# Where the experts' buffers start in their partitions: 96 bytes past a multiple of 512 in place of 384

## The chip, the cores and the metric

One core of a Trainium2 chip runs the whole program in one launch. The metric is the device time of that launch in microseconds, the median of several executions.

## The reference, cut to what matters

The program computes two blocks on a sequence of 256 tokens of width 1024, all in float32. The first block has two layers of mLSTM and retention; the second has two layers of convolution and banded attention, each followed by a feed-forward part, which is dense in the first layer and a mixture of eight experts in the second. The mixture is the part that the change touches:

```python
logits = t @ w_router + b_router            # t: 256 x 1024, 8 experts
top_val, top_idx = lax.top_k(logits, 2)
combine = sum(one_hot(top_idx) * softmax(top_val))
for e in range(8):
    out += combine[:, e:e+1] * ((silu(t @ w_gate[e]) * (t @ w_up[e])) @ w_down[e])
```

w_gate[e] and w_up[e] are 1024 x 3584, w_down[e] is 3584 x 1024. One expert has 42 MiB of weights, all eight 336 MiB.

## The kernel before, in words

**Split products.** Each float32 product is computed as three products of the type float32r. An operand x is split into a high part (x cast to float32r) and a low part (x minus the high part), and high by high, low by high and high by low are summed in PSUM. Weights come in units of 1 MiB, 2048 floats in each of 128 partitions: SP loads a unit into one of the slots of `raw` (line 529), ScalarE casts it to `whi` (line 739), VectorE subtracts to get `wlo` (line 1781), and TensorE multiplies. `whi` and `wlo` have three slots each. A unit is cast two units ahead of TensorE, and its cast waits until TensorE is done with the unit that held the slot.

**The experts.** For each expert, at most 128 chosen tokens are gathered (lines 1626 and 1648) into `xghi` and `xglo`. 28 units hold gate and up weights, 14 hold down weights. In both parts the tokens are the stationary operand, 128x128, and the weights are the moving one, 512 columns wide; each unit takes 12 products:

```python
mm(o, xghi[:, k, x], whi[:, u.hl, w], start=k == 0, stop=False)      # line 1682
mm(o, xglo[:, k, x], whi[:, u.hl, w], start=False, stop=False)       # line 1683
last = mm(o, xghi[:, k, x], wlo[:, u.hl, w], ...)                    # line 1684
```

Lines 1713 to 1715 are the same for down, with `thi` and `tlo` (the gated rows, turned by TensorE in line 1668 and taken out of PSUM by lines 1108 and 2451) as the stationary operand. That makes 8 x 28 x 12 = 2688 products of gate and up and 8 x 14 x 12 = 1344 of down, 4032 together. The result of an expert, scaled, is split into `ehi` and `elo` and spread back to the tokens' places with `pickT` as the moving operand, 256 columns (lines 1656 and 1657). An extra pass for experts with more than 128 tokens exists and runs only if there are such.

**Everywhere else** the weights are mostly the stationary operand, 128x128, and activations the moving one, 256 columns: `hhi` and `hlo` in lines 1161 to 1163, `yhi`, `fhi` and `y2hi` and their low parts in lines 1216 to 1218. In lines 1202 to 1204 the roles are the other way round, also with 256 columns. The sums of squares in line 1233 and the transposes are plain float32.

**Places.** Buffers are allocated one behind the other in each partition by `sb(...)`, and stacks that are closed give their place back, so later stages lie over earlier ones. Some small buffers (`half_line_h`, `half_line_c`, `half_line_y`, 32 bytes each) hold nothing and only move what follows. Worked out from the sizes, the starts modulo 512 bytes are: `raw`, `whi`, `wlo` 128; `hhi`, `hlo` 160; `acc` and `pickT` 192; `yhi`, `fhi`, `y2hi` and their low parts 224; `thi`, `tlo`, `htok`, `xghi`, `xglo`, `mg`, `ma`, `pick`, `ehi`, `elo` 384. Each slice that a product reads starts a whole number of 512 bytes behind its buffer's start, so every product has its buffers' residues. Taking the moving operand's start minus the stationary one's, modulo 512, gives one number for each family of products:

| products | moving | stationary | difference |
|---|---|---|---|
| 1161-1163 | `hhi`, 256 columns | `whi` | +32 |
| 1202-1204 | `whi`, 256 | `hhi` | -32 |
| 1216-1218 | `yhi`, `fhi`, `y2hi`, 256 | `whi` | +96 |
| 1648 | `pick`, 256 | `hhi` (tokens) | +224 |
| 1656, 1657 | `pickT`, 256 | `ehi`, `elo` | +320 |
| 1682-1684, 1713-1715 | `whi`, `wlo`, 512 | `xghi`, `thi` | +256 |

**Order.** Each engine's order is written out by hand and kept by semaphores; no planner decides it. `lrow`, a 256-float buffer for the router's logits, lies in `acc[:, 2]`; ScalarE writes it (line 1071) and TensorE reads it (line 1610) once, before the experts.

Of the kernel before, what the change touches and what calls it, by code (L numbers as in the profile page):

```python
# [5 lines left out]
F32 = mybir.dt.float32  # L6
# [6 lines left out]
P = 128  # L13
S = 256
# [24 lines left out]
FE = 3584  # L39
# [20 lines left out]

UW = 2048
HALF_LINE = 8
RAW = 6
HALF = 3
MOE_SLOTS = (3, 4, 5, 2, 0, 1)
# [32 lines left out]
S_MOE = S_B3 + UNIT_L2  # L98
assert S_MOE % HALF == 2 and A_MIX1 + ADA_MIX[1] == ADA_UNITS and (2 * HEAD_UNITS) % HALF == 0 and JOB_UNITS % RAW == 0 and JOB_UNITS % HL == 0 and ADA_TURN[0] % HALF == 0 and ADA_TURN[1] % HALF == 0
FREE0, DONE0 = HALF, 1  # L100
# [25 lines left out]
class Unit:  # L126
# [17 lines left out]
    @property  # L144
    def raw(self):
        return self.n % HALF if self.n < S_MOE else MOE_SLOTS[(self.n - S_MOE) % RAW]

    @property
    def loads(self):
        slots = HALF if self.n < S_MOE else RAW  # L150
        if self.n < S_MOE:
            first = self.n // HALF
        else:
            first = (self.n - S_MOE) // RAW + ((S_MOE + HALF - 1 - self.raw) // HALF if self.raw < HALF else ADA_UNITS // HALF - sum(HALF + i % HALF == self.raw for i in ADA_SPARE))
        return self.turn * (16 * self.per // slots) + (16 * first + 16) if self.per else 16 * first + 16
# [104 lines left out]
def two_block_model(nc, x, positions, consts, c, w_ada, b_ada, norm_g, w_in, conv_w, conv_b, b_igate, b_fgate,  # L260
# [7 lines left out]
    with ctx:  # L268
        def sb(name, shape, dt=F32, stack=ctx):
            return stack.enter_context(nc.sbuf_tensor(name, shape, dt))  # L270

        def sem(name):
            return ctx.enter_context(nc.semaphore(name))


        raw = sb("raw", [P, RAW, UW])
        whi = sb("whi", [P, HL, UW], F32R)
# [3 lines left out]

        sb("half_line_h", [P, HALF_LINE])
        hhi = sb("hhi", [P, KD, S], F32R)
        hlo = sb("hlo", [P, KD, S], F32R)
        sb("half_line_c", [P, HALF_LINE])
        cst = sb("cst", [P, C_BEFORE])
# [16 lines left out]
        acc = sb("acc", [P, HALF, S], F32, ba)  # L303
        sb("half_line_y", [P, HALF_LINE], F32, ba)

# [89 lines left out]
        ba.close()  # L395
        bm = ExitStack()
        pickT = sb("pickT", [P, S], F32R, bm)
        sb("rest_of_acc", [P, 2 * S + HALF_LINE], F32, bm)
        sb("half_line_t", [P, 5 * HALF_LINE], F32, bm)
        thi = sb("thi", [P, FE // P, P], F32R, bm)  # L400
        tlo = sb("tlo", [P, FE // P, P], F32R, bm)
        htok = sb("htok", [P, 2, D], F32, bm)
# [2 lines left out]
        mg = sb("mg", [P, 2, 512], F32, bm)  # L405
# [2 lines left out]
        moe = h  # L408
        wr = sb("wr", [P, KD, NE], F32, bm)
        rb = sb("rb", [P, 1], F32, bm)  # L410
        lrow = acc[:, 2]
        lg = rstd[:, 0:24 * NE].rearrange("p (a t e) -> p a t e", a=12, t=2)
        comb = sb("comb", [P, 2, NE + 1], F32, bm)
        combhl = sb("combhl", [P, 2, NE + 1, 2], F32R, bm)
# [5 lines left out]
        otok, hthi, htlo = (x[:, :, :].rearrange("p (t k) s -> p t (k s)", t=2) for x in (h, hhi, hlo))  # L420
        bm.close()
        be = ExitStack()
        sb("before_htok", [P, S + 2 * S + HALF_LINE + 5 * HALF_LINE + 2 * FE], F32, be)
        ehi = sb("ehi", [P, D], F32R, be)
        elo = sb("elo", [P, D], F32R, be)
        be.close()
# [17 lines left out]

        raw_in = [sem(f"raw_in{i}") for i in range(RAW)]
        c_in, rows1_in = sem("c_in"), sem("rows1_in")
# [2120 lines left out]
```

How the kernel before makes its waits and increments, by code:

```python
    def wait(self, back=0):  # L247
        v = self.n - back
        self.eng.wait_ge(self.sem, self.turn * self.per + v if self.per else v)
# [269 lines left out]
        @block.sync  # L519
# [6 lines left out]
            def load(u, src, k):  # L526
                sp.wait_ge(raw_free, u.free(1 - (HALF if u.n < S_MOE else RAW)))
                sp.dma_start(raw[:, u.raw, :].rearrange("p (k n) -> p k n", k=k), src).then_inc(raw_in[u.raw], 16)
# [1 line left out]
            def ada_load(a, block, l, at):  # L531
                if a.n >= ADA_START:
                    last = Ada(a.n - HALF, 0)
                    if ADA_START <= last.n < A_MIX0 or A_FF <= last.n < A_MIX1:
                        sp.wait_ge(ada_free, last.sums())
                    else:
                        sp.wait_ge(ada_done, last.count())
                elif a.n >= HALF:
                    sp.wait_ge(ada_done, a.n - HALF - len(ADA_SPARE) + 1)
                w = (w_ada, w_ada_2)[block][l].rearrange("(k p) n -> p k n", p=P)
                sp.dma_start(raw[:, a.raw, :].rearrange("p (k n) -> p k n", k=KD), w[:, :, bass.ds(at * 256, 256)])\
                    .then_inc(raw_in[a.raw], 16)
# [64 lines left out]
                        load(u, w[:, 4 * half:4 * half + 4, 512 * c:512 * c + 512], 4)  # L608
                    else:
                        f = 2 * (j - JOB_UP)
                        load(u, wd[:, f:f + 2, :], 2)
            sp.wait_ge(ada_done, ADA_UNITS)
            with sp.Fori(0, NE) as e:
                job_loads(e, e, S_MOE, range(JOB_UNITS))
```

## Time and profile before

| | us |
|---|---|
| median of three executions | 2103.86 (2103.12 to 2104.84) |
| profiled execution, its own time | 2104.48 |
| span of the profiled execution | 2102.6 |
| TensorE busy | 2055.7 (98%) |
| VectorE busy | 1766.0 (84%) |
| ScalarE busy | 1322.5 (63%) |
| mean transfer rate over the span | 283 GB/s |

The profile lists, for each engine, how long it was busy; a chain of waits from the last instruction back to the first; groups of equal instructions with their mean duration; and the data transfers. Durations of matrix products run from a product's start to its modelled end, and products overlap: the next one starts before the former one's end. How far apart starts are is read from the start times. The experts' stage runs from about 1117 us to 2089 us of the span.

### The profile page before, as it was taken

Reading aid. Unit: us, or ns where it says so; the run is one execution under the profiler, and the core shown is the slowest. Engines: PE = TensorE matmul, PEld = TensorE weight load, DVE = VectorE, ACT = ScalarE, POOL = GpSimd, SP = SyncE. Lnnn points to the kernel's source line nnn. Section 1 sums busy time; section 2 is a strip of 40 time slices with the busy share of each in tenths; the row PEclk is TensorE's granted clock in tenths of the full one; section 3 lists DMA queues with packets and bytes.
Section 4 is the critical chain, followed back from the end, with each engine's and each line's share of the span. In section 5 each row is a group of like instructions: output and inputs, shape, how many; then the busy total and the mean of one; then the engine's idle time right before and its main releaser. Section 6 shows DMA issues by size and latency. Waiting matters only on the chain.

```text
span 2102.6 us, 33818 instructions
## 1 busy us (share of the span) xinstructions
PE 2055.7 (98%) x13569; PEld 1833.1 (87%) x13569; DVE 1766.0 (84%) x2185; ACT 1322.5 (63%) x1265; POOL 30.5 (1%) x60
## 2 busy tenths in 40 slices
PE   7999999999999999999999999999999999999998
PEld 5999999999999889999878888888888888888887
DVE  4898976888759878888878888898898889898887
ACT  3655655566645663435757777777777777777774
POOL 3000000000000000000000000000000000000000
PEclk8999999999999999999999999999999999999999
DMA  9887865676656369987447999999999999999994
GB/s 297 252 260 239 250 211 161 221 220 198 216 183 218 128 213 307 312 323 227 141 164 268 360 354 360 373 367 344 362 358 374 361 343 367 368 365 355 355 359 187
DMA packets 356161, 595.07 MB, mean 283 GB/s; under 512 B 10376, under 2 KB 201368, under 8 KB 356008
## 3 DMA queue, kind: packets, MB, share of 16 engines
q1 hardware_dynamic: 352864, 586.92, 80.8%
q0 software_dynamic: 2752, 5.86, 1.1%
q8 instruction: 110, 1.80, 0.4%
q14 instruction: 43, 0.35, 0.0%
q10 hardware_dynamic: 392, 0.13, 0.0%
HBM read 591.80 MB, written 4.22 MB: 283 GB/s over the span
## 4 chain that ended last, share of the span: by engine, by line
PE 85%; DVE 8%; ACT 3%; DMA 2%; issue 2%; SPq 0%; POOL 0%; DVEq 0%; POOLq 0%; ACTq 0%
PE ps L1682 9%; PE ps L1684 9%; PE ps L1683 9%; PE ps L1161 6%; PE ps L1163 6%; PE ps L1162 6%; PE ps L1715 5%; PE ps L1714 5%; PE ps L1713 5%; PE ps L1216 3%; PE ps L1217 3%; PE ps L1218 3%; DVE wlo L1781 2%; PE ps L1202 1%; PE ps L1203 1%
## 5 line engine op out<-in xcount | busy, mean ns | idle before, releaser
L1781 DVE TENSOR_TENSOR wlo<-raw,whi 128x2048 fp32r<-128x2048 f32 x485 | 1108.6, 2287 | 190.4 <-ACT whi L739 189.8
L739 ACT CAST whi<-raw 128x2048 fp32r<-128x2048 f32 x485 | 926.5, 1911 | 363.2 <-PE ps L1684 123.6
L1161 PE MATMUL ps<-hhi,whi 128*128 128x256 f32 x1360 | 388.0, 285 | 0.5 <-DVE wlo L1781 0.5
L1163 PE MATMUL ps<-hhi,wlo 128*128 128x256 f32 x1360 | 380.4, 280 | 0.0
L1162 PE MATMUL ps<-hlo,whi 128*128 128x256 f32 x1360 | 380.3, 280 | 0.0
L1682 PE MATMUL ps<-whi,xghi 128*128 128x512 f32 x896 | 354.6, 396 | 0.8 <-DVE wlo L1781 0.8
L1684 PE MATMUL ps<-wlo,xghi 128*128 128x512 f32 x896 | 349.7, 390 | 0.0
L1683 PE MATMUL ps<-whi,xglo 128*128 128x512 f32 x896 | 349.1, 390 | 0.0
L1161 PEld LDWEIGHTS ps<-hhi,whi 128*128 128x128 f32 x1360 | 256.5, 189 | 7.6 <-issue 7.3
L1162 PEld LDWEIGHTS ps<-hlo,whi 128*128 128x128 f32 x1360 | 256.5, 189 | 0.3
L1163 PEld LDWEIGHTS ps<-hhi,wlo 128*128 128x128 f32 x1360 | 256.4, 189 | 0.0
L1684 PEld LDWEIGHTS ps<-wlo,xghi 128*128 128x128 f32 x896 | 168.2, 188 | 36.0
L1682 PEld LDWEIGHTS ps<-whi,xghi 128*128 128x128 f32 x896 | 168.3, 188 | 34.4 <-DVE wlo L1781 2.4
L1683 PEld LDWEIGHTS ps<-whi,xglo 128*128 128x128 f32 x896 | 168.5, 188 | 32.2
L1713 PE MATMUL ps<-whi,thi 128*128 128x512 f32 x448 | 175.2, 391 | 0.0
L1715 PE MATMUL ps<-wlo,thi 128*128 128x512 f32 x448 | 174.9, 390 | 0.0
L1714 PE MATMUL ps<-whi,tlo 128*128 128x512 f32 x448 | 174.6, 390 | 0.0
L1837 DVE SCALAR_TENSOR_TENSOR acc<-raw,cact,acc 128x256 f32<-128x256 f32 x324 | 132.7, 477 | 0.0
L1715 PEld LDWEIGHTS ps<-wlo,thi 128*128 128x128 f32 x448 | 84.1, 188 | 17.7
L1714 PEld LDWEIGHTS ps<-whi,tlo 128*128 128x128 f32 x448 | 84.1, 188 | 17.0
L1713 PEld LDWEIGHTS ps<-whi,thi 128*128 128x128 f32 x448 | 84.1, 188 | 16.9
L1202 PE MATMUL ps<-whi,hhi 128*128 128x256 f32 x320 | 91.8, 287 | 0.0
(407 smaller groups left out, 3011.5 us busy)
## 6 DMA issues: line engine op xcount, KB each, us to landing
raw<-in_moe_w_gate_dram SPq DMA_DIRECT2D x112, 1024.0 KB, 6.2
raw<-in_moe_w_up_dram SPq DMA_DIRECT2D x112, 1024.0 KB, 6.4
raw<-in_moe_w_down_dram SPq DMA_DIRECT2D x112, 1024.0 KB, 5.1
raw<-in_w_in_dram SPq DMA_DIRECT2D x92, 1024.0 KB, 5.4
raw<-in_w_ada_dram SPq DMA_DIRECT2D x69, 1024.0 KB, 7.8
raw<-in_w_out_dram SPq DMA_DIRECT2D x24, 1024.0 KB, 5.1
raw<-in_ffn_w_gate_dram SPq DMA_DIRECT2D x11, 1024.0 KB, 9.1
raw<-in_ffn_w_up_dram SPq DMA_DIRECT2D x11, 1024.0 KB, 9.1
```

Of the source, the lines that this page charges most:

```text
L739: nc.scalar.copy(whi[:, u.hl, :], raw[:, u.raw, :]).then_inc(hi_ready, 1)
L1161: mm(ps2[u.bank][:, j], whi[:, u.hl, w], hhi[:, k], start=k == 0, stop=False)
L1162: mm(ps2[u.bank][:, j], whi[:, u.hl, w], hlo[:, k], start=False, stop=False)
L1163: last = mm(ps2[u.bank][:, j], wlo[:, u.hl, w], hhi[:, k], start=False, stop=k == KD - 1)
L1682: mm(o, xghi[:, k, x], whi[:, u.hl, w], start=k == 0, stop=False)
L1683: mm(o, xglo[:, k, x], whi[:, u.hl, w], start=False, stop=False)
L1684: last = mm(o, xghi[:, k, x], wlo[:, u.hl, w], start=False, stop=k == KD - 1)
L1713: mm(o, thi[:, f], whi[:, u.hl, w], start=f == 0, stop=False)
L1714: mm(o, tlo[:, f], whi[:, u.hl, w], start=False, stop=False)
L1715: last = mm(o, thi[:, f], wlo[:, u.hl, w], start=False, stop=f == FE // P - 1)
L1781: V.tensor_tensor(wlo[:, u.hl, :], raw[:, u.raw, :], whi[:, u.hl, :].bitcast(F32), ALU.subtract).then_inc(raw_free, 1)
L1837: last = V.scalar_tensor_tensor(sums[k % 2], w[:, k], cact[:, block, k:k + 1], sums[k % 2], ALU.mult, ALU.add)
```

## The change

All buffers of the experts' stage that lie behind `pickT` begin 288 bytes earlier modulo 512 (1824 bytes earlier in all): at 96 in place of 384. The two unused buffers between `pickT` and `thi` (520 + 40 floats) become one of 104 floats. `pickT` stays at 192, the weights at 128. `ehi` and `elo`, which lie over `htok`, move with it. As `thi` now covers the place of `acc[:, 2]`, `lrow` is put into the first 256 floats of `mg`. The difference of the experts' products (moving minus stationary) becomes 128 - 96 = +32, that of lines 1656 and 1657 +96, that of line 1648 96 - 160 = -64. No instruction, wait or order is added, taken away or moved.

```diff
 HALF_LINE = 8
+T_PAD = 104
 RAW = 6
...
         pickT = sb("pickT", [P, S], F32R, bm)
-        sb("rest_of_acc", [P, 2 * S + HALF_LINE], F32, bm)
-        sb("half_line_t", [P, 5 * HALF_LINE], F32, bm)
+        sb("before_thi", [P, T_PAD], F32, bm)
         thi = sb("thi", [P, FE // P, P], F32R, bm)
...
-        lrow = acc[:, 2]
+        lrow = mg[:, 0, 0:S]
...
         be = ExitStack()
-        sb("before_htok", [P, S + 2 * S + HALF_LINE + 5 * HALF_LINE + 2 * FE], F32, be)
+        sb("before_htok", [P, S + T_PAD + 2 * FE], F32, be)
         ehi = sb("ehi", [P, D], F32R, be)
```

## Rows read from the trace of the kernel before

**Rows 1.** The page: engine shares, the 40 slices, the chain's shares by engine.

```profile
PE 2055.7 (98%) x13569; PEld 1833.1 (87%) x13569; DVE 1766.0 (84%) x2185; ACT 1322.5 (63%) x1265; POOL 30.5 (1%) x60
...
PE   7999999999999999999999999999999999999998
...
PE 85%; DVE 8%; ACT 3%; DMA 2%; issue 2%; SPq 0%; POOL 0%; DVEq 0%; POOLq 0%; ACTq 0%
```

**Rows 2.** Busy time in two stretches: experts, down part (us, engines, clock, DMA share, GB/s).

```profile
1117.00:2089.00 972.00, 970.31 (x4504) 804.84 (x4504) 862.62 (x544) 704.38 (x474) 0.00 (x0) 1.00 0.98 355
1325.00:1355.00 30.00, 30.00 (x134) 24.82 (x134) 25.80 (x13) 21.07 (x11) 0.00 (x0) 1.00 1.01 378
```

**Rows 3.** Waits from 1200 to 2050 us: waiting instruction, releaser, total us, times, longest.

```profile
ACT whi L739 <- PE ps L1684: 108.2, 139, 1.6
DVE wlo L1781 <- ACT whi L739: 95.5, 159, 1.4
ACT whi L739 <- PE ps L1715: 88.8, 97, 1.9
```

**Rows 4.** The experts' product groups of the page: busy us, mean ns, idle before.

```profile
L1682 PE MATMUL ps<-whi,xghi 128*128 128x512 f32 x896 | 354.6, 396 | 0.8 <-DVE wlo L1781 0.8
L1684 PE MATMUL ps<-wlo,xghi 128*128 128x512 f32 x896 | 349.7, 390 | 0.0
L1683 PE MATMUL ps<-whi,xglo 128*128 128x512 f32 x896 | 349.1, 390 | 0.0
L1713 PE MATMUL ps<-whi,thi 128*128 128x512 f32 x448 | 175.2, 391 | 0.0
L1715 PE MATMUL ps<-wlo,thi 128*128 128x512 f32 x448 | 174.9, 390 | 0.0
L1714 PE MATMUL ps<-whi,tlo 128*128 128x512 f32 x448 | 174.6, 390 | 0.0
```

**Rows 5.** TensorE from 1504 to 1511 us: start us, duration us, product.

```profile
1504.21 0.39 PE L1682 MATMUL ps<-whi,xghi 128*128 128x512 f32 x1
...
1507.38 0.39 PE L1684 MATMUL ps<-wlo,xghi 128*128 128x512 f32 x1
1507.62 0.60 PE L1668 MATMUL ps<-cst,ma 128*128 128x128 f32 x4
1507.97 0.48 PE L1682 MATMUL ps<-whi,xghi 128*128 128x512 f32 x1
1508.28 0.40 PE L1683 MATMUL ps<-whi,xglo 128*128 128x512 f32 x1
...
1510.14 0.39 PE L1682 MATMUL ps<-whi,xghi 128*128 128x512 f32 x1
```

**Rows 6.** Products by line: duration ns min/median/max, first and last start us.

```profile
L1684 PE MATMUL ps<-wlo,xghi x896: 387/389/398, 1111.3 to 2050.1; 128*128 128x512 f32 x180
L1715 PE MATMUL ps<-wlo,thi x448: 388/389/398, 1192.0 to 2088.7; 128*128 128x512 f32 x150
L1161 PE MATMUL ps<-hhi,whi x1360: 277/280/470, 48.1 to 1041.6; 128*128 128x256 f32 x195
L1204 PE MATMUL ps<-wlo,hhi x320: 274/280/288, 56.8 to 1025.1; 128*128 128x256 f32 x160
L1218 PE MATMUL ps<-fhi,wlo x176: 278/282/286, 900.2 to 966.8; 128*128 128x256 f32 x176
L1648 PE MATMUL ps<-pick,hhi x64: 278/282/283, 1198.0 to 1960.0; 128*128 128x256 f32 x64
L1656 PE MATMUL ps<-pickT,ehi x64: 279/282/419, 1256.9 to 2092.9; 128*128 128x256 f32 x64
```

**Rows 7.** TensorE: a stretch of 256-column products, and one of plain float32.

```profile
564.18 0.28 PE L1163 MATMUL ps<-hhi,wlo 128*128 128x256 f32 x1
...
566.98 0.28 PE L1163 MATMUL ps<-hhi,wlo 128*128 128x256 f32 x1
...
636.85 3.62 PE L1233 MATMUL ps<-h,gsq 128*128 128x256 f32 x16
```

**Rows 8.** VectorE's subtraction of 512 columns at either residue: busy us, mean ns.

```profile
L2451 DVE TENSOR_TENSOR tlo<-ps,thi 128x512 fp32r<-128x512 f32 x56 | 38.2, 683 | 0.0
L2314 DVE TENSOR_TENSOR flo<-fa,fhi 128x512 fp32r<-128x512 f32 x11 | 7.5, 684 | 0.0
```

## The prediction

> **What bounds the kernel now.** I read the page's busy shares first, then the chain, then the experts' stage by itself, and last the single products. The page shows TensorE busy for 98% of the span in all 40 slices and 85% of the chain on it [rows 1]. In the experts' stage, 972 us long, TensorE is busy for 970.31 us at full clock, and VectorE for 862.62 us, 89% [rows 2]. The waits say who leads: ScalarE's cast waits for TensorE to give a slot back, 197 us in total in that stage, and the largest of the others is VectorE's wait for the cast; no cast waits for a transfer [rows 3]. So a nanosecond more or less on each of the experts' products arrives in the end time nearly whole, and nothing else that the change touches can.
>
> Busy time hides how fast products follow each other, so I take starts. In rows 5, from 1504.21 to 1507.38 us there are 14 steps: 3.17 us / 14 = 226.4 ns from start to start, with durations of 389 ns. Duration minus step is 163 ns. The 256-column products show the same difference: 24 steps from 564.18 to 566.98 us are 116.7 ns each, under a median of 280 [rows 7, 6]. Plain float32 products too: 16 of them take 3.62 us, their last start lies 3.62 - 0.38 = 3.24 us behind the first, 216 ns a step, at 379 ns each [rows 7]. So I read a duration minus 163 as the cost of a product in a stream, and can use the groups' durations as a ruler at one nanosecond. Over 4032 products, one nanosecond is 4.0 us of the kernel.
>
> **The change part by part.** It takes away no instruction and no wait. What it can alter is how the reads of the moving operand and of the next stationary operand meet in a partition, which depends on the difference of their places.
>
> *The experts' 4032 products, difference +256 to +32.* The median is 389 ns, the least 387 [rows 6]: most of them run in one settled rhythm, 226.4 ns. Does the settled rhythm depend on the difference? No row shows 512 columns at +32, so I bound it by the 256-column families. Their medians are 280 at +32, 280 at -32, 282 at +96, +224 and +320 [rows 6], so the difference is worth about 2 ns there. Their shortest, apart from one at 274, are 277 to 279, that is 114 to 116 ns a step. Half of the experts' 226.4 is 113.2: for each column they are already as fast as the quickest products of any family at any difference. I take that as a floor that the place does not move, and the settled rhythm as unchanged: 0 us.
>
> *The unsettled ones.* After the transposes the rhythm is disturbed: from 1508.28 to 1510.14 us 8 steps take 1.86 us, 232.5 ns each [rows 5]. The six groups are busy for 354.6 + 349.1 + 349.7 + 175.2 + 174.9 + 174.6 = 1578.1 us [rows 4]; 4032 x 0.389 = 1568.4; 9.7 us are above the settled duration. Of these, 56 products that follow a transpose directly last about 0.48 us, 0.09 more than 0.39 [rows 5]: 5.0 us, which is the transposes' own time. The rest, 4.7 us, is what the disturbed rhythm costs. With another difference it can go to nothing, or become the rule: all products at 232.5 would cost 4032 x 6.1 = 24.6 us. The bounds are thus -4.7 and +24.6 us while the floor holds, and I take 0, since the row nearest to it is the settled one, at which most of the stage runs now.
>
> If the floor does not hold, the nearest lower row is plain float32 at 216 ns: 10.4 x 4032 = 41.9 us less.
>
> *The 128 spreading products (+320 to +96) and the 128 gathering ones (+224 to -64).* The families differ by 2 ns in their medians [rows 6], so 256 x 2 = 0.5 us either way; taken as 0.
>
> *ScalarE and VectorE* write the moved buffers at an odd multiple of 32 bytes in place of a multiple of 64. `flo` already lies so (224) and `tlo` does not (384), and VectorE takes 684 and 683 ns for them [rows 8]: 0. If ScalarE's or VectorE's pieces grew by 1%, they have slack: VectorE's 862.62 of 972 us [rows 2]. The transfers of weights keep their places. `lrow` in `mg` is written and read once, by the same instructions behind the same waits, and `mg` is first used by the experts afterwards: 0.
>
> The sum is 0 with bounds of -42.4 and +25.1 us (both with the 0.5). The profiled execution took 2104.48 us, its span 2102.6 and 1.9 around it; the median is 2103.86, 0.6 lower, and I apply the sum to the median: 2103.9.
>
> Two rules of the Trainium skill bear on this. The page SBUF — State Buffer (section "SBUF: two separate sides") says that TensorE has ports of its own and never waits on another engine, and in its table of paths that the weight load has a second, independent read port. By that rule no difference of places could cost anything. The trace does not quite agree: the same products at the same clock last 389 ns or up to 398 [rows 6], depending on what ran before them. The page TensorE: Matmul & The Clock Gate (section "Back-to-back issue gap") gives N/2.4 + 2.5 ns at full clock, an estimate of 215.8 ns for 512 columns. [...]
>
> **The rivals.** The reader can tell them apart by the median duration alone.
>
> *Slower: at +32 the rhythm does not settle.* The place is every expert product; the mechanism is that the load of the next tokens and the moving weights meet again in each product. For it: the only family at +32 does not run at its own shortest, 277, but at 280 in the median, 3 ns more [rows 6], while at +256 the experts show no such excess. Carried over, 4032 x 3 = 12.1 us: 2116. At the disturbed 232.5 ns it would be 2128. Against it: with 512 columns the weight load has twice the time, and the disturbed rhythm was seen to die out. It decides from 1 ns a product on.
>
> *Faster, a little: the difference carries over as it stands.* At +32 the 256-column products are 2 ns better than at +96, +224 and +320. If +256 is like these and half-hidden in the 389, the experts gain 2 to 3 ns: 8 to 12 us, 2094. Against it: at -32 the median is 280 as well, and the floor argument above.
>
> *Faster, much: the floor is no floor.* 41.9 us less, 2062, if all the excess over plain float32 goes. VectorE would then be busy for 862.6 of 930 us, 93%, and the transfers run at 355 x 972/930 = 371 GB/s, below the 378 that the down part shows [rows 2], so neither forbids it. Against it: none of the five 256-column families comes near half of 216.
>
> **How the numbers follow.** Forecast, rhythm unchanged: 0.45. Slower: 0.28. A little faster: 0.19. Much faster: 0.08. A change of less than 0.2%, 4.2 us, is what a measurement of this kernel can hardly tell from none. The forecast's own range is 2099 to 2109; I leave 0.02 of its chance beyond 4.2 us on either side. So faster is 0.19 + 0.08 + 0.02 = 0.29, same 0.41, slower 0.28 + 0.02 = 0.30. The range is 2090 to 2120: it takes in the little gain and the 12.1 us loss, and leaves out the much faster case (0.08) and the fully disturbed one (some 0.07).
>
> **What would show it.** Right: lines 1684 and 1715 keep a median of 389 ns, the six groups' busy time stays within 5 us of 1578.1, and the experts' stage is 968 to 976 us long. The slower rival shows a median of 392 or more; the faster ones 386 to 387, or 379. The counts of rows 6 for lines 1161 and 1218 must not move at all. If the six groups' sum changes by more than 5 us and the end time does not follow, my reading that nothing waits beside TensorE is wrong; if the time moves with all durations as before, something outside the products did it.

## The result and the profile after

The changed kernel is slower: 2124.43 us in the median of four executions (2123.39 to 2125.58) against 2103.99 for the kernel before beside it. The ratio is 1.0100, 95% interval 1.0087 to 1.0112. The forecast was 2103.9 with a range of 2090 to 2120, so the time lies outside it, on the side of the rival "at +32 the rhythm does not settle". Of all executions of the kernels below, one, of e9_even256, ran at a lower mean granted clock than the rest (0.92 in place of 0.99) and took 2137.23 us; it is in the ratio given there.

The page of the kernel after, to be laid beside [rows 1]:

```profile
span 2121.5 us, 33818 instructions
PE 2075.2 (98%) x13569; PEld 1830.6 (86%) x13569; DVE 1766.7 (83%) x2185; ACT 1321.6 (62%) x1265; POOL 30.5 (1%) x60
```

The instructions are as many as before. VectorE's and ScalarE's busy times are within 1 us of what they were; TensorE is busy for 2075.2 us in place of 2055.7, 19.5 more, and the span is 18.9 longer. The experts' stage alone, as in [rows 2], ends 18.5 us later (the last product of line 1715 starts at 2107.2 us, before at 2088.7) and has hardly a gap in TensorE's time:

```profile
1117.00:2107.00 990.00, 989.37 (x4494) 802.45 (x4493) 860.70 (x542) 701.70 (x472) 0.00 (x0) 1.00 0.98 348
```

The six groups of [rows 4] in the kernel after (line, products, count, busy us, mean ns, idle before):

```profile
L1682 PE MATMUL ps<-whi,xghi 128*128 128x512 f32 x896 | 358.7, 400 | 0.6 <-DVE wlo L1781 0.6
L1684 PE MATMUL ps<-wlo,xghi 128*128 128x512 f32 x896 | 353.9, 395 | 0.0
L1683 PE MATMUL ps<-whi,xglo 128*128 128x512 f32 x896 | 353.7, 395 | 0.0
L1713 PE MATMUL ps<-whi,thi 128*128 128x512 f32 x448 | 177.7, 397 | 0.0
L1714 PE MATMUL ps<-whi,tlo 128*128 128x512 f32 x448 | 176.9, 395 | 0.0
L1715 PE MATMUL ps<-wlo,thi 128*128 128x512 f32 x448 | 176.9, 395 | 0.0
```

They sum to 1597.8 us against 1578.1: 19.7 us, which is the whole of the loss within what the two profiles can tell. (Counted from the first expert product to the last, the stage is 21.1 us longer; it began 2.6 us earlier in this execution.) Every group has grown by 4 to 6 ns in its mean. The durations by line, beside [rows 6]:

```profile
L1684 PE MATMUL ps<-wlo,xghi x896: 388/396/400, 1108.7 to 2067.6; 128*128 128x512 f32 x180
L1715 PE MATMUL ps<-wlo,thi x448: 388/394/400, 1191.0 to 2107.2; 128*128 128x512 f32 x150
L1161 PE MATMUL ps<-hhi,whi x1360: 277/280/470, 48.4 to 1039.8; 128*128 128x256 f32 x195
L1218 PE MATMUL ps<-fhi,wlo x176: 278/282/286, 899.9 to 966.5; 128*128 128x256 f32 x176
```

Before, the median lay at the short end (389 of 387 to 398), now it lies at the long end (396 and 394 of 388 to 400). The longest hardly grew: what was the exception after a disturbance is now the rule. Lines 1161 and 1218, whose buffers did not move, have the durations they had. TensorE's starts, as in [rows 5], show the rhythm (start us, duration us, product):

```profile
1503.71 0.40 PE L1682 MATMUL ps<-whi,xghi 128*128 128x512 f32 x1
1503.94 0.39 PE L1683 MATMUL ps<-whi,xglo 128*128 128x512 f32 x1
1504.17 0.40 PE L1684 MATMUL ps<-wlo,xghi 128*128 128x512 f32 x1
...
1506.97 0.40 PE L1684 MATMUL ps<-wlo,xghi 128*128 128x512 f32 x1
1507.21 0.28 PE L1656 MATMUL ps<-pickT,ehi 128*128 128x256 f32 x1
```

From 1503.71 to 1506.97 us there are 14 steps: 232.9 ns each, where the kernel before had 226.4. In the down part, from 1328.82 to 1339.79 us, 47 steps take 10.97 us, 233.4 ns each, with nothing else between them. The step does not fall with time: this is a settled rhythm too, only a slower one. The single steps, read from the starts in ns, are 230 to 235, where the kernel before has 226 and 227 in turn; those average 226.7, and the 226.4 of the prediction is the same rhythm read from starts that are rounded to 10 ns.

The settled step grew by 6.6 ns, and 4032 times that is 26.6 us, more than the 20.4 lost: the kernel before also paid for its disturbed stretches, and the slow rhythm does not pay for them a second time. Over all expert products that follow each other directly, the mean step went from 227.5 to 233.2 ns.

### The profile page after: what moved, and what is told of

The parts are those of the page before. It is cut to its first block, busy times and chain, and to the rows that moved or that the text cites. A ratio compares the mean times of both kernels' runs of the same rounds, so it can differ in the third digit from the quotient of the medians.

```text
span 2121.5 us, 33818 instructions
## 1 busy us (share of the span) xinstructions
PE 2075.2 (98%) x13569; PEld 1830.6 (86%) x13569; DVE 1766.7 (83%) x2185; ACT 1321.6 (62%) x1265; POOL 30.5 (1%) x60
## 4 chain that ended last, share of the span: by engine, by line
PE 86%; DVE 7%; ACT 3%; issue 2%; DMA 2%; SPq 0%; POOL 0%; DVEq 0%; POOLq 0%; ACTq 0%
PE ps L1682 9%; PE ps L1684 9%; PE ps L1683 9%; PE ps L1161 6%; PE ps L1163 6%; PE ps L1162 6%; PE ps L1715 5%; PE ps L1714 5%; PE ps L1713 5%; PE ps L1216 3%; PE ps L1217 3%; PE ps L1218 3%; DVE wlo L1781 2%; PE ps L1202 1%; PE ps L1203 1%
## 5 line engine op out<-in xcount | busy, mean ns | idle before, releaser
L1683 PE MATMUL ps<-whi,xglo 128*128 128x512 f32 x896 | 353.7, 395 | 0.0
L1713 PEld LDWEIGHTS ps<-whi,thi 128*128 128x128 f32 x448 | 84.0, 188 | 19.5
```

The costliest lines, as they stand in the source:

```text
L1713: mm(o, thi[:, f], whi[:, u.hl, w], start=f == 0, stop=False)
```

## The experiments

Theory A: only the difference of the two starts (moving minus the next stationary operand, modulo 512 bytes or less) sets the step. Its rivals were the place as such, the alignment of the stationary operand alone, and `lrow`. Each kernel below is compared with the kernel before on its own chip. Unless said otherwise it is the kernel after with one number changed.

**e1_r384: the old residue in the new layout.**

```diff
-T_PAD = 104
+T_PAD = 176
```

> The changed layout (one pad in place of two, lrow in mg), but with the pad at 176 floats, so that the experts' buffers start at 384 modulo 512 bytes again, 1536 bytes lower than before. Theory A (only the difference of starts, moving minus next stationary, modulo 512, sets the step): back to 226.4 ns a step, median duration 389, time 2104 +-3 us. Rival B (lrow in mg, or the lower place as such, costs it): stays at 233.3 ns and 2124 us.

Measured: 2103.12 us against 2102.94, ratio 1.0003 (0.9993 to 1.0012). The median of line 1684 is 389 ns again. So `lrow` and the lower place cost nothing that shows within 0.1%; B falls.

**e2_shift224: everything moved by 224 bytes, all differences kept.**

```diff
+        sb("front", [P, 56])
         raw = sb("raw", [P, RAW, UW])
```

> The changed kernel with 224 bytes of nothing ahead of raw, so that every buffer starts 224 bytes further: tokens and gated rows at 320 (a multiple of 64), weights at 352. All differences are those of the changed kernel (+32). Theory A: step 233.3 ns, 2124 us. Rival C (the stationary operand's start at an odd multiple of 32 bytes costs it, whatever the moving one's): step 226.4 to 227, about 2104 us. Lines 1161 to 1163 keep 116.7 ns by A.

Measured: 2124.89 us against 2102.94, ratio 1.0104 (1.0084 to 1.0124). Line 1684 of the other kernels is line 1685 here:

```profile
L1685 PE MATMUL ps<-wlo,xghi x896: 388/394/400, 1111.3 to 2070.1; 128*128 128x512 f32 x180
```

With the tokens at a multiple of 64 bytes the loss is all there. Where the stationary operand starts modulo 64 bytes does not matter by itself; C falls. That the common place does not matter at all rests on this one shift.

**e3_down96: the new difference for the down products only.**

```diff
+        sb("before_tok", [P, 72], F32, bm)
         htok = sb("htok", [P, 2, D], F32, bm)
...
-        sb("before_htok", [P, S + T_PAD + 2 * FE], F32, be)
+        sb("before_htok", [P, S + T_PAD + 2 * FE + 72], F32, be)
```

> Gated rows (thi, tlo) at 96, and 288 bytes of nothing behind them, so that the gathered tokens (xghi, xglo) and ehi's neighbours start at 384: only the down products have the new difference. Theory A: lines 1713 to 1715 at 396 to 394 ns and 233.3 a step, lines 1682 to 1684 at 389; 1344 of 4032 products x 6.9 ns = 9.3 us less the third part of the old unsettled cost (1.5): about 2112. Rival D (the loss comes from one stage's order, or from the two meeting): 2104 or 2124.

Measured: 2110.26 us against 2102.94, ratio 1.0033 (1.0018 to 1.0048), 7.3 us for a third of the products, a little over a third of 20.4 and somewhat less than the 8 expected. Lines 1684 and 1715 are 1685 and 1716 here:

```profile
L1685 PE MATMUL ps<-wlo,xghi x896: 387/389/398, 1111.3 to 2056.3; 128*128 128x512 f32 x180
L1716 PE MATMUL ps<-wlo,thi x448: 388/394/397, 1191.9 to 2096.0; 128*128 128x512 f32 x150
```

The two parts are independent: one keeps 389, the other has 394. D falls, and the loss is bound to the products that have the difference.

**e4_r128, e5_r64, e6_r160, e7_r32: other differences.** One edit each:

```diff
-T_PAD = 104
+T_PAD = 112    # e4: tokens at 128, difference 0
+T_PAD = 96     # e5: at 64, +64
+T_PAD = 120    # e6: at 160, -32
+T_PAD = 216    # e7: at 32, +96
```

> Pad of 112 floats: tokens and gated rows at 128, the same residue as the weights, difference 0. Theory A says only that the step depends on the difference; if the unsettled rhythm belongs to small positive differences (the two readers start in step and stay so), 0 is as slow as +32 or slower: 233 ns or more, 2124 us or more. Rival E (32 bytes granularity of a store's halves: an odd difference costs, an even one does not): 226.4 ns, 2104 us.

> Pad of 96 floats: tokens and gated rows at 64, difference +64. So far 0 and +256 gave 226.4 ns a step and +32 gave 233.3. Theory F (what counts is the difference modulo 64 bytes: 0 settles, 32 does not): 226.4 ns, medians of 389, about 2103 us. Rival G (the fast places are far from a small positive difference, with a period of 256 bytes or more): between 226.4 and 233.3 or slower, 2110 us or more.

> Pad of 120 floats: difference -32. Theory F: 233.3 ns a step, medians 394 to 396, 2123 to 2125 us, as +32. Rival G (only small positive differences are slow, since the faster stream must start ahead of the slower one to meet it): 226.4 ns, 2103 us.

> Pad of 216 floats: tokens and gated rows at 32, difference +96, which is 32 modulo 64 but lies 64 bytes from the changed kernel's. Theory F: 233.3 ns, 2123 to 2125 us. Rival G: another value, nearer 226.4.

Measured, with +32 and +256 from above; the step is the mean of several, taken from the down part's starts between 1329 and 1334 us (e1 and e4: 18 steps in 4.08 us, e5: 19 in 4.35, e6 and e7: 18 in 4.20; after: 47 in 10.97 from 1329 to 1340):

| difference | step, ns | time, us | before beside it | ratio (95%) |
|---|---|---|---|---|
| 0 (e4) | 226.7 | 2102.83 | 2102.94 | 1.0000 (0.9989 to 1.0010) |
| +256 (e1) | 226.7 | 2103.12 | 2102.94 | 1.0003 (0.9993 to 1.0012) |
| +64 (e5) | 228.9 | 2108.97 | 2103.97 | 1.0025 (1.0014 to 1.0037) |
| +32 (after) | 233.4 | 2124.43 | 2103.99 | 1.0100 (1.0087 to 1.0112) |
| -32 (e6) | 233.3 | 2124.72 | 2103.97 | 1.0104 (1.0085 to 1.0122) |
| +96 (e7) | 233.3 | 2126.98 | 2103.97 | 1.0114 (1.0096 to 1.0133) |

Line 1715 in e4, e5, e6 and e7, in this order, one kernel each:

```profile
L1715 PE MATMUL ps<-wlo,thi x448: 388/389/398, 1191.5 to 2088.3; 128*128 128x512 f32 x150
```

```profile
L1715 PE MATMUL ps<-wlo,thi x448: 388/392/397, 1192.7 to 2094.6; 128*128 128x512 f32 x150
```

```profile
L1715 PE MATMUL ps<-wlo,thi x448: 389/395/397, 1191.0 to 2106.8; 128*128 128x512 f32 x150
```

```profile
L1715 PE MATMUL ps<-wlo,thi x448: 388/397/399, 1194.1 to 2110.8; 128*128 128x512 f32 x150
```

The first and the last start of the stretches of e4 (18 steps), e5 (19) and e6 (18):

```profile
1329.80 0.39 PE L1713 MATMUL ps<-whi,thi 128*128 128x512 f32 x1
...
1333.88 0.39 PE L1713 MATMUL ps<-whi,thi 128*128 128x512 f32 x1
```

```profile
1329.61 0.39 PE L1713 MATMUL ps<-whi,thi 128*128 128x512 f32 x1
...
1333.96 0.39 PE L1714 MATMUL ps<-whi,tlo 128*128 128x512 f32 x1
```

```profile
1329.64 0.40 PE L1715 MATMUL ps<-wlo,thi 128*128 128x512 f32 x1
...
1333.84 0.40 PE L1715 MATMUL ps<-wlo,thi 128*128 128x512 f32 x1
```

The three odd multiples of 32 bytes are alike: about 233 ns. 0 and +256 are alike, down to the unsettled steps. That is what theory F says. But F also wanted 226.4 at +64, and it got 228.9: there one step in three is 226 ns, the others 229 and 232. So "modulo 64" holds for the slow differences and fails for the even ones: F stands as a rule for which of the differences tried to avoid, not as the whole law. Of the rivals, E (odd against even multiples of 32) fails at the same point and in the same way. G's step at +64, between the two, did come, but G falls all the same, since -32 is as slow as +32 and +96 is no faster.

Theory A is not the whole law either. The three lines of a triple have one and the same difference modulo 512 bytes, yet in e5 their steps are 226, 229 and 232 ns in turn, and in e7 232, 237 and 231. Something beyond the difference modulo 512 has a part of a few ns in each step; what it is, no run shows. The difference sets the mean.

**e9_even256: the same differences for 256 columns.** The kernel before with other pads:

```diff
-        sb("half_line_h", [P, HALF_LINE])
...
-        sb("half_line_c", [P, HALF_LINE])
+        sb("half_line_c", [P, 2 * HALF_LINE])
...
-        sb("half_line_y", [P, HALF_LINE], F32, ba)
+        sb("half_line_y", [P, 6 * HALF_LINE], F32, ba)
...
-        sb("rest_of_acc", [P, 2 * S + HALF_LINE], F32, bm)
-        sb("half_line_t", [P, 5 * HALF_LINE], F32, bm)
+        sb("rest_of_acc", [P, 2 * S + 6 * HALF_LINE], F32, bm)
```

> The kernel before with the 256-column families put on differences that are fast with 512 columns: hhi and hlo at 128 (lines 1161 to 1163 and 1202 to 1204: difference 0), yhi, fhi, y2hi and their low parts at 384 (lines 1216 to 1218: +256); the experts' buffers stay at 384. Theory H (one rule for all widths: 0 and +256 are free of stalls): steps fall from 116.7, 118.3 and 120.8 ns to 113.3, half of 226.7; 5000 x 3.4 + 1680 x 7.5 = 30 us less, about 2074 us. Rival I (with 256 columns the load of the next stationary operand covers the whole product, and the best difference is another one): steps of 117 ns or more for these families, 2104 us or more.

Measured: 2110.22 us against 2103.03, ratio 1.0060 (1.0016 to 1.0103): slower. The execution of 2137.23 us pulls that ratio up; the two medians alone give 1.0034, 7.2 us, and the other five executions (2109.09 to 2111.86) all lie above the nine of the kernel before (2101.59 to 2104.33). Lines 1163, 1204 and 1218 are 1161, 1202 and 1216 here; PEld is the load of the stationary operand:

```profile
L1161 PEld LDWEIGHTS ps<-hhi,wlo x1360: 187/192/192, 48.8 to 1049.5; 128*128 128x128 f32 x195
L1161 PE MATMUL ps<-hhi,wlo x1360: 278/283/288, 48.9 to 1049.7; 128*128 128x256 f32 x195
L1202 PE MATMUL ps<-wlo,hhi x320: 279/283/283, 57.5 to 1032.8; 128*128 128x256 f32 x160
L1216 PE MATMUL ps<-fhi,wlo x176: 280/283/283, 907.5 to 973.9; 128*128 128x256 f32 x176
```

```profile
563.74 0.28 PE L1160 MATMUL ps<-hlo,whi 128*128 128x256 f32 x1
...
566.74 0.28 PE L1161 MATMUL ps<-hhi,wlo 128*128 128x256 f32 x1
```

25 steps in 3.00 us: 120.0 ns, where +32 has 116.7 [rows 7]. Taken over the whole of each family (the mean distance of successive starts, those over 140 ns left out as interruptions), this is what the change of difference did:

| lines | before | e9 |
|---|---|---|
| 1161-1163 | +32: 116.9 ns | 0: 119.8 ns |
| 1202-1204 | -32: 118.3 | 0: 119.8 |
| 1216-1218 | +96: 119.9 | +256: 119.8 |

The differences that are best with 512 columns are worse than +32 and -32 with 256, also in lines 1202 to 1204, where the weights move and the tokens are stationary as in the experts. So it is the width, not the role, that turns the order of 0 and -32 round. Lines 1216 to 1218 did not get slower, though the median duration of line 1218 (`fhi`) rose from 282 to 283 ns. H falls; I holds for the steps of 117 ns or more, its reason is not shown. The load's median went from 187 or 188 to 192 ns in all three families. The steps would make about 13 us (4080 x 2.9 ns and 960 x 1.5 ns) and 7.2 arrived; TensorE's idle time fell by 4 us, the rest was not traced.

**e8_rows32: +32 where it is good.** The kernel before, with the products of lines 1216 to 1218 put on the difference of lines 1161 to 1163 (`pickT` moves too, which puts the 128 products of lines 1656 and 1657 on +256):

```diff
-        eps = sb("eps", [P, 1])
-        eps2 = sb("eps2", [P, 1])
-        ln_eps = sb("ln_eps", [P, 1])
+        three = sb("three", [P, 3])
+        eps, eps2, ln_eps = (three[:, i:i + 1] for i in range(3))
...
-        sb("half_line_t", [P, 5 * HALF_LINE], F32, bm)
+        sb("half_line_t", [P, 7 * HALF_LINE], F32, bm)
...
-        sb("before_htok", [P, S + 2 * S + HALF_LINE + 5 * HALF_LINE + 2 * FE], F32, be)
+        sb("before_htok", [P, S + 2 * S + HALF_LINE + 7 * HALF_LINE + 2 * FE], F32, be)
```

> The kernel before, with eps, eps2 and ln_eps in one buffer, which moves all behind them 64 bytes down: yhi, fhi and y2hi with their low parts start at 160, difference +32 in place of +96; the experts' buffers are held at 384. The 1680 products of lines 1216 to 1218 stand at about 120.8 ns a step, lines 1161 to 1163 with +32 at 116.7 to 117. If a 256-column family's step depends on the difference alone: 1680 x 3.5 = 5.9 us less, medians of 280 in place of 282, about 2097 us against 2103. If by the rule of 512 columns (modulo 64, where +96 and +32 are alike): no change.

Measured: 2099.09 us (11 executions) against 2103.97 (19), ratio 0.9977 (0.9968 to 0.9986): 4.9 us less than the kernel before, where 5.9 were expected. Line 1218 is 1217 here, and the starts are those of line 1215 to 1217:

```profile
L1217 PE MATMUL ps<-yhi,wlo x256: 276/279/283, 291.9 to 633.8; 128*128 128x256 f32 x128
L1217 PE MATMUL ps<-fhi,wlo x176: 276/281/281, 896.0 to 961.4; 128*128 128x256 f32 x176
```

```profile
740.15 0.28 PE L1216 MATMUL ps<-y2lo,whi 128*128 128x256 f32 x1
...
742.37 0.28 PE L1217 MATMUL ps<-y2hi,wlo 128*128 128x256 f32 x1
```

19 steps in 2.22 us are 116.8 ns. That is the step of lines 1161 to 1163: with 256 columns this family's step follows the difference, and +32 and +96 are not alike. Over the whole family the mean step fell from 119.9 to 117.0 ns, and 1680 x 2.9 ns is 4.9 us, all that was measured; the expectation had taken 120.8 for the step at +96. Between families the difference is not all: in the kernel after, line 1656 stands at +96 as well, and its 64 steps to line 1657 have a mean of 117.4 ns.

## Why the prediction was wrong, point by point

*That TensorE sets the pace of the experts' stage, and nothing waits beside it* was right: 19.7 us more in the six groups, 20.4 us more in the time. The other engines did no more work and waited longer; VectorE's wait for the cast, 95.5 us in [rows 3], is in the same stretch of the kernel after:

```profile
DVE wlo L1781 <- ACT whi L739: 110.9, 163, 1.5
```

*Duration minus 163 ns as a ruler* held to 1 ns for 512 columns (395 to 396 at 233). With 256 columns it is coarser than the differences in question: the median of line 1218 rose from 282 to 283 ns in e9 while the mean step of its family stayed (119.9 and 119.8 ns), because a median hides how the single durations spread.

*The settled rhythm does not depend on the difference: 0 us.* This is the step that failed. The prediction put it so: "I take that as a floor that the place does not move, and the settled rhythm as unchanged". That this rhythm is the least that 512 columns settle at held in every run; that the kernel would stay there did not follow. A floor says how much a change can gain, not that it loses nothing. Measured, the settled step went from 226.7 to 233.3 ns, and the change cost 20.4 us where the prediction had 0.

*Bounding the missing row by the 256-column families* was the error under it. Their medians showed 2 ns between the differences (3 by their mean steps, 116.9 to 119.9 ns), and +32 among the best. With 512 columns the spread is 6.6 ns, and +32 is among the worst. e4 and e9 show the two orders: difference 0 gives 226.7 ns at 512 columns, the least seen, and 120.0 at 256, which is 3.3 above +32.

*The row for "the floor is no floor"*, plain float32 at 216 ns, is of products with 256 columns [rows 7]. It is of another type and half the width, so it could not serve as a bound for the experts' products, nor half of it as one for the 256-column families.

*The bound of +24.6 us from the disturbed rhythm* was right and should have been weighed as a case of its own: 232.5 ns in [rows 5] is within 1 ns of the new settled step, and the measured loss is 83% of the bound. The prediction gave it 0.07 and let the range end at 2120, because it saw the disturbance die out. It dies out at +256; at +32 nothing shows that it does.

*The spreading and gathering products* were taken as 0 with 0.5 us around them, and nothing on record is against it. The means of the spreading ones are 288 and 287 ns before and 292 and 293 after, but e2, at the same difference as after, has 282 and 282, and e1, at that of before, 283 and 280: the profiles scatter more than the change. The gathering ones have medians of 281 in place of 282 and 280. *ScalarE, VectorE and `lrow`* at 0 were right as well (e1).

On the Trainium skill: the page SBUF — State Buffer (section "SBUF: two separate sides") calls the weight load's read port independent and sees contention among the engines only at the ports that VectorE and GpSimd share. The runs disagree with what the prediction drew from it, that no difference of places could cost anything: equal instructions at equal clock, with nothing changed but the distance between their two operands, take 226.7 to 233.4 ns a step. The page TensorE: Matmul & The Clock Gate (section "Back-to-back issue gap") gives N/2.4 + 2.5 ns, for 512 columns an estimate of 215.8 ns, for the gap of an isolated product, which the prediction did not say, and about 131 ns for a stream with 512 columns. The experts' float32r streams agree with neither; no difference tried came below 226.7.

What stays open is the mechanism. That the moving reads and the load's reads meet in the partition's memory would fit the facts that moving all buffers together costs nothing more (e2) and that the order turns round with the width (e9). It is not shown. In e9 the load became 4 ns longer, in the kernel after the loads kept 187 to 188 ns and the products grew; but the longer load is not by itself the price, since in lines 1216 to 1218 of e9 it grew too and the step did not. No run separated the two reads.

## What to carry to other kernels

For a stream of products whose next stationary operand is loaded beside them, place the buffers by their difference, and try it at the very width of the moving operand: of the differences tried, 0 or 256 bytes was best with 512 float32r columns, +32 with 256. Don't carry a good difference from one width to the other, and don't bound a missing case by families of another width. When a row shows a slow form of the same instruction that appears only after disturbances, price the case in which it becomes the rule, and leave it in the range.

## What the runs showed of the hardware that was not expected

The mean step takes few values: 226.7 ns at differences of 0 and 256, 228.9 at 64, 232.9 to 233.4 at 32, -32 and 96, all at 512 columns. At 256 columns the means are 116.9 ns at 32, 118.3 at -32, 119.8 at 0 and 256, and 119.9 at 96. No 512-column stream settled below 226.7 ns and no 256-column one below 116.7, against 216 ns for plain float32 with 256 columns [rows 7]. Moving all buffers together by 224 bytes changed nothing that could be measured (2124.89 us against 2124.43).
